# First weight slabs of the output projection and of the MLP, worked through singly instead of in pairs

## What is computed

```python
x = x + g1 * (jnp.concatenate([y_a, y_b, y_c], axis=-1) @ lp['w_out'])
h = _rmsnorm(x, lp['norm2_g']) * (1 + sc2) + sh2
x = x + g2 * (jnp.square(jax.nn.relu(h @ lp['mlp_w1'])) @ lp['mlp_w2'])
```

## Time and profile before

| | |
|---|---|
| time, median of 3 runs | 2178.71 us (2174.47 to 2181.6) |
| the profiled execution: its time, its span | 2176.15 us, 2174.3 us |
| TensorE matmul busy | 1866.1 us, 86% of the span, 19967 matmuls |
| VectorE busy | 1052.5 us, 48% |
| GpSimd busy | 726.4 us, 33% |
| ScalarE busy | 600.7 us, 28% |
| TensorE clock granted, mean | 0.925 of full speed |
| output projection, first matmul to the MLP's first matmul | 1219.55 to 1331.99 us |
| MLP, first up matmul to the end of the down products | 1331.99 to 2148.7 us |

### The profile page before, as it was taken

How to read it: one execution, slowest core, us unless ns; L and a number is a source line. 1 busy time by engine, 2 the same in 40 slices (tenths; PEclk the granted TensorE clock), 3 DMA queues, 4 the chain that set the end, 5 groups by cost and what they waited for, 6 DMA issues and landing times. The chain is left out here.

```text
span 2174.3 us, 48450 instructions
## 1 busy us (share of the span) xinstructions
PE 1866.1 (86%) x19967; PEld 1761.1 (81%) x19967; DVE 1052.5 (48%) x2012; ACT 600.7 (28%) x1322; POOL 726.4 (33%) x502
## 2 busy tenths in 40 slices
PE   4584999377997489999983699899999999999997
PEld 3582998366997278888872599899999999999997
DVE  1707210477733866667659525434344343434354
ACT  3501222233223455555630312101111020202022
POOL 1311343044333323223321050343435344343433
PEclk8795999688999799999995799999999999999998
DMA  8360111031120000000010210111201111111112
GB/s 312 130 238 24 30 48 22 20 91 51 39 94 27 4 7 4 4 4 4 3 52 29 111 44 10 39 49 34 61 25 53 40 38 48 29 48 34 54 34 112
DMA packets 148630, 114.11 MB, mean 52 GB/s; under 512 B 13018, under 2 KB 133361, under 8 KB 148093
## 3 DMA queue, kind: packets, MB, share of 16 engines
q1 hardware_dynamic: 148477, 111.86, 16.7%
HBM read 99.01 MB, written 12.84 MB: 51 GB/s over the span
## 5 line engine op out<-in xcount | busy, mean ns | idle before, releaser
L618 PE MATMUL bank<-YT_r,Z_r 128*128 128x384 f32 x2304 | 401.8, 334 | 0.0
L618 PEld LDWEIGHTS bank<-YT_r,Z_r 128*128 128x128 f32 x2304 | 399.1, 188 | 1.6 <-issue 1.1
L2592 DVE SCALAR_TENSOR_TENSOR XT<-bank,MOD,XT 128x384 f32 (+5 forms) x288 | 142.3, 515 | 326.5 <-PE bank L618 309.6
L618 PE MATMUL bank<-HT_r,W_r 128*128 128x384 f32 x1344 | 266.3, 340 | 11.2 <-PEq L111 7.8
L618 PEld LDWEIGHTS bank<-HT_r,W_r 128*128 128x128 f32 x1344 | 239.4, 190 | 12.7 <-issue 8.9
L2883 ACT ACTIVATE PAD<-PAD,up_bias 128x384 f32<-128x384 f32 (+2 forms) x128 | 65.2, 533 | 558.3 <-DVE PAD L2921 558.3
L596 POOL TENSOR_TENSOR Z_r<-Z,ones 128x512 fp32r<-128x512 f32 x64 | 87.4, 1366 | 297.7 <-DMA Z<-in_mlp_w 297.7
L618 PE MATMUL bank<-Z_r,W_r 128*128 128x388 f32 (+1 forms) x720 | 141.1, 338 | 7.8 <-POOL Z_r L602 7.8
L596 POOL TENSOR_TENSOR W_r<-Z,ones 128x1024 fp32r<-128x1024 f32 x32 | 78.3, 2448 | 202.5 <-DMA Z<-in_mlp_w 202.5
L618 PE MATMUL bank<-Z_r 128*128 128x388 f32 (+1 forms) x720 | 140.7, 337 | 0.0
L618 PEld LDWEIGHTS bank<-Z_r,W_r 128*128 128x128 f32 x720 | 127.2, 189 | 8.1 <-POOL Z_r L602 8.1
(11 more groups left out here) (429 smaller groups left out, 3358.4 us busy)
## 6 DMA issues: line engine op xcount, KB each, us to landing
Z<-in_w_mod SPq DMA_DIRECT2D x11, 2048.0 KB, 12.4
Z<-in_mlp_w SPq DMA_DIRECT2D x32, 512.0 KB, 4.3
Z<-in_mlp_w SPq DMA_DIRECT2D x64, 256.0 KB, 2.8
YT<-gate_rows_x SPq DMA_DIRECT2D x18, 384.0 KB, 4.2
YT<-in_w_in SPq DMA_DIRECT2D x12, 512.0 KB, 3.8
PAD<-in_w_in SPq DMA_DIRECT2D x10, 512.0 KB, 5.1
residual<-XT SPq DMA_DIRECT2D x3, 1536.0 KB, 11.4
XT<-residual SPq DMA_DIRECT2D x1, 4608.0 KB, 13.8
```

The costliest lines, as they stand in the source:

```text
L618: mm = nc.tensor.matmul(out, w[slot][:, k, :], x(k, g), start=(n == 0 and k == 0), stop=(n == 2 and k == self.blocks - 1))
L2592: ins = nc.vector.scalar_tensor_tensor(out=x, in0=S.PS[3 * slot + g][:, a:b], scalar=S.MOD[:, ds(col, 1), c:c + 1].rearrange("p a b -> p ( ...
```

## The change

Both stages are no longer built with `paired`. The output projection's iteration 0 calls `multiply` for slot 0 and then for slot 1. By the same flag, the consumers read slot 0's three banks first, and the load of iteration 1 into slot 0 waits for three finished tiles instead of five. `first_pair_pe` is written anew: slot 0's high-part products of all groups, the sums for the normalisation, slot 1's high-part products of groups 0 and 1, slot 0's low-part products, slot 1's high-part products of group 2, slot 1's low-part products. The number of matmuls, transfers and elementwise instructions is the same.

```diff
--- before.py
+++ after.py
@@ -2543,7 +2543,7 @@
     w_out = io["w_out"][0].rearrange("(k p) n -> p k n", p=P)
     high = slabs([lambda x: x[2], lambda x: x[3]], (S.PADr,))[0]
     S.dense = dense = Dense(S, "o", slabs([lambda x: x[:, 9, :], lambda x: x[:, 10, :]], (S.Z, S.Zr)),
-                            high, paired=True)
+                            high)
     with nc.Block() as block:
         @block.gpsimd
         def _(pool):
@@ -2599,7 +2599,7 @@
 
     nc, io = S.nc, S.io
     dense = S.dense
-    S.up = up = Dense(S, "up", slabs([lambda x: x[:, 8, P:], lambda x: x[:, 11, :]], (S.Z, S.Zr)), paired=True,
+    S.up = up = Dense(S, "up", slabs([lambda x: x[:, 8, P:], lambda x: x[:, 11, :]], (S.Z, S.Zr)),
                           lead=UpRows.LEAD)
     S.up_rows = rows = UpRows(S)
     w1 = io["mlp_w1"][0].rearrange("(k p) n -> p k n", p=P)
@@ -2645,8 +2645,9 @@
 
         @block.tensor
         def _(pe):
-            dense.multiply_pair(pe, group(S.HTr), group(S.YTr),
-                                lambda g: pe.wait_ge(left.sem, left.at(0, KB * (g + 1))))
+            for slot in range(2):
+                dense.multiply(pe, 0, slot, group(S.HTr), group(S.YTr),
+                               lambda g: pe.wait_ge(left.sem, left.at(0, KB * (g + 1))))
             with pe.Fori(1, 4) as i:
                 for slot in range(2):
                     dense.multiply(pe, i, slot, group(S.HTr), group(S.YTr))
@@ -2766,25 +2767,34 @@
 
     def first_pair_pe(pe):
 
-        products = ((up.high_r, rows_up.moving), (up.low_r, rows_up.moving), (up.high_r, group(S.HTr)))
+        def with_high(slot, g):
+            pe.wait_ge(up.split.sem, up.split.at(0, slot + 1))
+            pe.wait_ge(up.drained[g].sem, up.drained[g].last(0, slot + 1))
+            for n, w in enumerate((up.high_r, up.low_r)):
+                for k in range(KB):
+                    if k == KB - 1:
+                        pe.wait_ge(rows_up.rounded.sem, rows_up.rounded.at(0, (KB - 1) * NG + g + 1))
+                    nc.tensor.matmul(up.whole(slot, g), w[slot][:, k, :], rows_up.moving(k, g),
+                                     start=(n == 0 and k == 0), stop=False)
+
+        def with_low(slot, g):
+            pe.wait_ge(rows_up.left.sem, rows_up.left.at(0, KB * (g + 1)))
+            for k in range(KB):
+                mm = nc.tensor.matmul(up.bank(slot, g), up.high_r[slot][:, k, :], S.HTr[:, k, g * GRP:(g + 1) * GRP],
+                                      start=False, stop=(k == KB - 1))
+            mm.then_inc(up.summed.sem, 1)
+
         pe.wait_ge(rows_up.shift_low.sem, rows_up.shift_low.at())
         for g in range(NG):
-            for slot in range(2):
-                pe.wait_ge(up.split.sem, up.split.at(0, slot + 1))
-                pe.wait_ge(up.drained[g].sem, up.drained[g].last(0, slot + 1))
-                for n, (w, x) in enumerate(products[0:2]):
-                    for k in range(KB):
-                        if k == KB - 1:
-                            pe.wait_ge(rows_up.rounded.sem, rows_up.rounded.at(0, (KB - 1) * NG + g + 1))
-                        nc.tensor.matmul(up.whole(slot, g), w[slot][:, k, :], x(k, g), start=(n == 0 and k == 0), stop=False)
-            pe.wait_ge(rows_up.left.sem, rows_up.left.at(0, KB * (g + 1)))
-            for slot in range(2):
-                w, x = products[2]
-                for k in range(KB):
-                    mm = nc.tensor.matmul(up.bank(slot, g), w[slot][:, k, :], x(k, g), start=False, stop=(k == KB - 1))
-                mm.then_inc(up.summed.sem, 1)
-            if g == 0:
-                sums_pe(pe)
+            with_high(0, g)
+        sums_pe(pe)
+        for g in range(2):
+            with_high(1, g)
+        for g in range(NG):
+            with_low(0, g)
+        with_high(1, 2)
+        for g in range(NG):
+            with_low(1, g)
 
     def index(eng, x, lo, hi):
         return x if isinstance(x, int) else eng.snap(x, min_val=lo, max_val=hi)
```

## The result

The changed kernel took 2166.12 us (median of 6 runs, 2163.12 to 2168.82), the kernel before 2179.57 (2174.47 to 2182.15 in 6 runs). The ratio is 0.9938 with a 95% interval of 0.9923 to 0.9953. The forecast was 2165 in a range of 2160 to 2172.5. Timed twice more, the changed kernel gave 0.9955 (0.9938 to 0.9971) and 0.9938 (0.9919 to 0.9958).

A forecast was written before the change was run, and what follows sets the result against it. TensorE, never resting from 1376 to 2148 us, was taken as the bound. Gains of 4.98 + 2.52 + 4.7 = 12.2 us gave 2163.9 from the profiled 2176.15 or 2166.5 from the median 2178.71; 2165 was taken, range 2160 to 2172.5.

The forecast's parts named there:

- Output projection: Output projection: iteration 1 starts 4.98 us earlier and its first tile costs 2.52 us less, together 7.50 us.
- rival C: Entering the output projection's loop: a wait hidden under the old stall takes 2.4 to 5 us back, about 2169; chance 0.09.
- MLP, TensorE's side: MLP's second up iteration: TensorE idles 2.1 us instead of 7.76 and starts 5.86 us earlier.
- the walk-through: MLP's first up iterations: step-by-step timing of matmuls, load and VectorE's chain, GpSimd's eight instructions included; chain ends at 1395.1.
- MLP, VectorE's side: First down products: VectorE's chain decides, group 2 starts at 1395.2 instead of 1399.9, a gain of 4.7 us.
- The blocking by GpSimd: MLP's first up tiles: GpSimd's eight instructions stretch VectorE's chain by 6.5 us in all; 3.3 us before.
- The rule used for it: MLP's first up tiles: each blocked VectorE instruction ends 0.4 us after the GpSimd one in its way.
- A: MLP: blocking is mild and TensorE decides, gaining 5.8 to 7.5 us there, about 2163 in all; chance 0.22.
- B: MLP: 10 to 15 us of blocking, TensorE waits 4 to 9 us before the down products, about 2171; chance 0.12.
- D: SyncE's queue: something else holds it, loads go out no earlier, time stays about 2178; chance 0.04.
- E: MLP: without the stalls as rests TensorE's clock drops for a stretch; 50 us of it gives 2191; chance 0.03.
- The sum: Whole kernel: 4.98 + 2.52 + 4.7 = 12.2 us gained over output projection and MLP.

The follow-up runs named there:

- after: The changed kernel itself, both parts, against the kernel before: 2166.12 us, ratio 0.9938.
- after_again: The same changed kernel, timed again beside the others against the kernel before: ratio 0.9955.
- after_fill: Changed kernel plus 12 matmuls with unused results in TensorE's wait ahead of the MLP's second up iteration: ratio 0.9957 to the kernel before.
- mlp_only: Only the MLP's first pair unpaired and reordered, output projection as in the kernel before: ratio 0.9984 to that kernel.
- pool_busy: Changed kernel plus four GpSimd instructions that nobody waits for, right behind its eight splits in the MLP: ratio 0.9956 to the kernel before.

## Why the prediction was right

**Output projection: 7.5 us forecast.** From the stage's first matmul on, the MLP starts 6.99 us earlier in the profile, 6.24 and 6.23 in the two others. All of the shortfall is the stage's first tile, which ran at the lower clock for longer (6.17, 6.88 and 6.95 us against 5.62). With that taken off it is 7.54, 7.50 and 7.56. The load left 14.8 us after the first matmul (14.25 forecast, and 0.55 of slow tile). The low parts were never late. Iteration 3 kept its margin of 0.65 us (slab split at 1298.82, wanted at 1299.47), and no gap at the loop's entry came (rival C).

**MLP, TensorE's side: 5.86 us forecast, 5.32 measured.** The wait was 2.23 us where 2.1 was forecast. The rest is the point at which the load can leave, 22.3 us after the stage's first matmul and not 21.8. The six eights ahead of the sums took 0.17 us longer than in the walk-through. The four behind them took 5.93 us and not 5.55, chiefly because the first eight there takes 1.7 us, not 1.4 (1339.27 to 1340.98 after, and as long before): a term mis-sized.

**MLP, VectorE's side: the third group 4.7 us earlier forecast, 3.48 measured.** The mechanism is as written: no reserve, two waits of 0.65 us, the group released by the chain. The blocking by GpSimd adds up to 6.9 us (the five long instructions shown and two of 0.8 us, against 0.56 each), forecast 6.5. The rule used for it, that a blocked instruction ends 0.4 us after the GpSimd one, held in all seven cases to 0.02 us. What the walk-through had wrong is when GpSimd works: it let the eight instructions follow each other directly, but they came in two parts with 2.56 us between them. It also left out that in the kernel before two more instructions were blocked (1.42 and 0.83 us, at 1376.70 and 1378.85), so that the blocking there was 4.4 us and not 3.3. The chain began at 19.5 us behind the stage's first matmul, not 19.0, and ended at 64.3, not 63.1. So the 1.2 us too much are 0.5 for the late first tile, 0.4 of blocking, and 0.3 because twelve tiles without the blocking take 37.9 us, not 37.6. In the two profiles where the clock stayed up ahead of the MLP the third group is at 62.8, 5.2 us earlier than before, but 1.4 of that is the luck of the first two eights.

**Which rival.** A would have needed the clock or TensorE's work to matter at the down products: from the second up iteration to the third group `after`, `after_again`, `after_fill` and `mlp_only` show 33.0, 32.9, 32.9 and 32.9 us whatever the clock. B's large blocking didn't come; what it would take is shown by `pool_busy`. D and E are out by the rows above (load issued in time; clock 1.00 in the MLP).

**The sum: 12.2 us forecast, 10.5 to 11.4 in the traces' stretch, 9.1 to 13.5 in the medians.** The mean of the three medians' differences is 11.6, beside 11.1 in the traces, which is 1 us under the forecast. From 2179.57 us the traces' gain leads to 2168.2 to 2169.1; that the first timing came out at 2166.12, so near to 2165, was partly luck of the runs.

## What to carry to other kernels

Pairing tiles for an early start delays the point at which any one weight buffer comes free; count when the next load can leave before choosing the order, and finish one buffer's tiles completely if the load, the split and the next use fill more than one tile's time. When a stall of the busiest engine is taken out, look at the reserve of the chain behind it: here VectorE had 5.9 us, and the change used it up. An engine off the critical path (GpSimd's splits) can stretch that chain just by being moved beside it, so walk the chain through with the moved work in place.

## What the runs showed of the hardware that was not expected

After the same pause the granted clock doesn't always do the same. The output projection's first tile, behind 6.3 to 6.4 us of idle time, took between 5.62 and 6.97 us over fourteen profiles. Behind the 2.4 us ahead of the MLP, the first two eights took 2.90 us in four profiles (clock kept) and 4.1 to 4.45 us in the other ten. A stretch that begins behind such a pause is therefore uncertain by about 1.5 us in a single profile, more than one of the effects studied here, and has to be compared at equal clock. The same holds for the 2.2 to 2.3 us ahead of the second up iteration: in `after` and `pool_busy` the clock fell to 0.50 once TensorE worked again, in `after_again` and `mlp_only` it stayed at 1.00. What decides it isn't shown.

A VectorE instruction with two SBUF inputs that meets a running GpSimd instruction is held until that one is over, whatever its own length. In the profiles of before and after all eleven stretched ones end 0.41 or 0.42 us behind a GpSimd instruction, whether that made them 0.83 or 2.50 us long. The multiplication that reads a bank (line 2921 before, 2931 after) was never longer than 0.56 us.
